# Forget-gate sums a slot later, drains ahead of a split, a second head-norm bank and sums placed later in a two-block fp32 transformer kernel

## The chip, the cores and the metric

One core of one Trainium2 chip runs the whole program. The metric is the device time of one launch in microseconds, taken as the median of several runs; smaller is better. The engines are TensorE (PE in the profile, with its weight loads as PEld), VectorE (DVE), ScalarE (ACT), GpSimd (POOL) and SyncE (SP, which here only issues DMAs). Each engine runs its own queue in order, and engines wait for each other by semaphores.

## The reference

Two transformer blocks over 256 tokens of width 1024, in float32, batch 1:

```python
def first_block(...):
    mod = silu(c) @ w_ada + b_ada                      # shift, scale, gate, twice
    u = rms_norm(x, ln1) * (1 + scale1) + shift1
    x = x + gate1 * mixer_sublayer(u, ...)             # gated conv + SSD scan, 32 heads
    u2 = rms_norm(x, ln2) * (1 + scale2) + shift2
    x = x + gate2 * (square(relu(u2 @ w_up)) @ w_down)
    return rms_norm(x, final_norm)

def second_block(...):
    fq, fk, fv, fg, dq, dk, dv = split(modulate(x) @ w_in)
    # q and k are normalised per head of 64; log_f = log_sigmoid(fg + b_f), its cumulative
    # sum over the tokens biases the 8 forget-gate ("fox") heads; 4 differential heads
    x = x + g1 * (concat(fox_out, diff_out) @ w_out)
    y = (silu(h2 @ w_gate) * (h2 @ w_up)) @ w_down
    return x + g2 * y
```

In the mixer, `dt = softplus(... + dt_bias)` steps the scan and `dt * a` is summed cumulatively over the tokens. The scan's output `y` times `silu(z)` is normalised in 8 groups of 256 channels before it meets `w_ssm_out`.

## The kernel before

Everything is kept transposed: channels on the 128 partitions, tokens along the row. `plan()` lays the weight products out as one list of steps. A step is one weight tile of 1024 rows by 256 columns (1 MB), made of two halves (`nb` 0 and 1) of 128 output columns. Each float32 product is three matmuls on numbers split into a high and a low part, so a half is 8 blocks x 3 = 24 matmuls, and a step 48.

Every engine's program walks the same list, `for n in range(NS)` and `for nb in range(NB)`; what it does there is its order in its queue, written out by hand. For a step n, SP brings the tile into one of three `raw` buffers, ACT makes `w_hi` (`split_hi`), DVE makes `w_lo` (`split_lo`), in general two steps ahead. PE takes a bank of PSUM (`take` waits until the previous content has been read out), multiplies, and signals `acc_ready` for each half; ACT and DVE then read ("drain") the bank. Three banks `acc0` to `acc2` go round, with the small banks M0 to M4 for everything else.

The steps in order, with the names that are used below: `xbc` 0 to 15 (scan inputs; `X0`), `cc`/`cx`/`cb` 0 to 3, two pairs `gc`/`co`, `z` 0 to 7 (`Z0`), two more pairs `gc`/`co`, then four times `gs`, `so`, `so`, then `wo` 0 to 3, `up` 0 to 15 (`U0`), `dn` 0 to 3 with four steps each (`D_LAST` is the last), `dq` 0 (`I0`), `dk` 0, `fg` (`FG`, 8 columns only), `dq` 1, `dk` 1, `fq` 0, `fk` 0, `fq` 1, `fk` 1, `dv` 0 and 1, `fv` 0 and 1, `o2` 0 to 3, `gt`/`u2` alternating (`G0`), `d2`.

The places that the change touches:

- **dt**: after half 1 of `xbc` 3 PE computes the 32 dt rows; ACT copies them; PE transposes them (L1355); DVE adds the bias (`dt_z`, L1617); after step `SOFT_AT` (`xbc` 5) ACT and DVE share the softplus (L801 to L804 and L1440 to L1449).
- **z_sum**: eight sums over partitions (L1305) of squares that POOL has added in pairs (L665), one for each step from `z` 2 on.
- **Late norms**: the first two steps of `up` and of `gt`/`u2` multiply a not yet normalised input (`gxh`, `gxl`); `x_sum` (L1080, L1082) adds the squares between their products, ACT makes the inverse root `mx` (L753, L754), and DVE applies it.
- **Tail of dn**: `x_sum_ahead` (L1056 to L1059) adds the first seven blocks' squares, which POOL has summed in `rt` (L613), and `x_sum(2)` (L1073 to L1076) the last one's, followed by `keep_busy(7)`, fill matmuls.
- **Head norms**: after half 0 of the step behind each q or k step PE sums squares per head into M0 (L1339); ACT takes the root (L753, L754), DVE reads M0 again (L1693) and scales q or k (to L1702).
- **Forget gate**: softplus after step `FG + 2` (`dk` 1) ends in `dta`; PE's cumulative sums into M4 (L1371 to L1374); ACT copies them out (L1011); DVE writes `fcum` and `fcum_t` (L1708 to L1712).
- **attn_slot**: `at` counts the halves from `dq` 0 on. Scores (L1257 to L1262) come in slots 6, 8, 12, 14, 16, 18, 20 and 22, and DVE and ACT handle the softmax in the same slots.

Of the kernel before, what the change touches and what calls it, by code (L numbers as in the profile page):

```python
# [34 lines left out]
HD = 64  # L35
# [158 lines left out]
def build(nc, a, out):  # L194
# [36 lines left out]
    for k, kind in enumerate(("up", "gt")):  # L231
        for m in range(2):
            LATE[start_of[kind] + m] = 2 * k + m
    LATE_NORM = (1, 4)
    GAIN_AT = {1: 1, 2: 2, 4: 3}
    NARROW, N_SETTLE = 32, 6
# [23 lines left out]
    with ExitStack() as ctx, ExitStack() as programs:  # L260
# [216 lines left out]
        def pv_bank(c):  # L477

            return PV_BANK[c if c < 4 else 4 + (c - 4) // 2]

        def split_late(n):

            return I0 <= n < start_of["o2"]
# [225 lines left out]
        def _(act):  # L709
# [162 lines left out]
            for n in range(NS):  # L872
# [3 lines left out]
                if n == 1:  # L876
                    act.wait_ge(S("dt_in"), 16)
                    act.activation(dt_hi[:, :, :], dt_raw[:, :, :], ACT.Copy).then_inc(S("dt_hi"), 1)
                if (s.kind, s.j) in (("wo", 2), ("dn", 3), ("o2", 2)) and s.last:
                    log_exp_table()  # L880
# [11 lines left out]
                for nb in range(NB):  # L892
# [60 lines left out]
                    if nb == 0 and prev in ("dq", "dk", "fq", "fk"):  # L953
                        jq += 1
                        act.wait_ge(S("qsum_done"), jq)
                        if jq > 1:
                            act.wait_ge(S("qk_done"), NB * (jq - 1))
                        inverse_root(qr, M0[:, :], HD, "qroot")

# [46 lines left out]
                    if n == FG + 1 and nb == 0:  # L1006
                        act.wait_ge(S("acc_ready"), steps[FG].g + NB)
                        act.activation(cv[0:8, 0, :], BANK[steps[FG].banks[0]][0:8, 0:T], ACT.Copy).then_inc(S("fg_t"), 1)
                    if n == FG + 3 and nb == 1:
                        act.wait_ge(S("fc_done"), 1)  # L1010
                        act.activation(fcum_t[0:2 * HEADS, P:3 * P], M4[0:2 * HEADS, T:2 * T], ACT.Copy)\  # L1011
                           .then_inc(S("fcum_hi"), 1)
# [29 lines left out]
        def _(pe):  # L1042
# [113 lines left out]
            def products(n, nb):  # L1156

                size = steps[n].group
                if steps[n].kind == "fg":
                    for i in range(4 * nb, 4 * nb + 4):  # L1160
                        product_part(n, 0, i)
                elif n in PAIRED:
                    if nb == 0:
                        for i0, i1 in ((0, PAIRED[n]), (PAIRED[n], KB)):
                            for b in range(NB):
                                for i in range(i0, i1):
                                    product_part(n, b, i)
                elif size == 1:
                    for i in range(steps[n].kts):
                        if n == D_LAST and nb == NB - 1 and i == KB - 2:  # L1170
                            x_sum_ahead()
                        product_part(n, nb, i)
                        if n in SETTLE_AT and nb == 0 and i == 0:
                            settle(n)
                if size > 1 and nb == 0:
                    if size == 3:
                        for i in range(6):
                            first_part(0, 0, i)
                            first_part(0, 1, i)
                            if i < 5:  # L1180
                                keep_busy(3)
                        for i in range(6):
                            first_part(1, 0, i)
                            first_part(1, 1, i)
                        for i in range(6, KB):
                            for m, b in ((0, 0), (0, 1), (1, 0), (1, 1)):
                                first_part(m, b, i)
                    order = [(m, b, i) for i in range(KB) for m in range(n + NAT * (size == 3), n + size) for b in range(NB)]
                    if n in LATE:
                        order = [(m, b, i) for m in (n, n + 1) for i in range(KB) for b in range(NB)]  # L1190
                    for m, b, i in order:
                        if n in LATE and (m, b, i) == (n, 0, 3):
                            x_sum(LATE_NORM[LATE[n] // 2])
                        product_part(m, b, i)
# [115 lines left out]
            for n in range(NS):  # L1310
                s = steps[n]
                for nb in range(NB):
                    products(n, nb)
                    if nb == 0 and 2 <= n - Z0 < 10:
                        z_sum(n - Z0 - 2)
# [19 lines left out]
                    if nb == 0 and n and steps[n - 1].kind in ("dq", "dk", "fq", "fk"):  # L1335
                        take("M0")
                        pe.wait_ge(S("qsq"), NB * (jq + 1))
                        jq += 1
                        pe.matmul(M0[:, :], blk64[:, :], sq[:, 2:4, :].rearrange("p a b -> p (a b)"), start=True, stop=True)\  # L1339
                          .then_inc(S("qsum_done"), 1)  # L1340
                        free["M0"] = ("qsum_read", jq)
                    if split_late(n):
                        attn_slot(NB * (n - I0) + nb)
                    if n == 3 and nb == 1:
# [6 lines left out]
                        ins.then_inc(S("dt_mm"), 1)  # L1351
                    if n == 4 and nb == 1:
                        pe.wait_ge(S("dt_t"), 1)
                        for t in range(TT):
                            ins = pe.transpose(M0[:, T + t * HEADS:T + (t + 1) * HEADS], gt[0:HEADS, 0, t * P:(t + 1) * P],  # L1355
                                               ident[0:HEADS, 0:HEADS])
                        ins.then_inc(S("dt_tr"), 1)
                        free["M0"] = ("dt_z", 1)
                    if n == FG + 2 and nb == 0:
# [4 lines left out]
                        ins.then_inc(S("fg_tr"), 1)  # L1364
                    if n == FG + 3 and nb == 1:
                        pe.wait_ge(S("nlf_done"), 1)
# [9 lines left out]
                        free["M4"] = ("fcum_done", 2)  # L1376
                if s.kind == "dn" and s.j == 3 and s.last:
                    x_sum(2)
                    keep_busy(7)
# [6 lines left out]
        def _(dve):  # L1386
# [165 lines left out]
            for n in range(NS):  # L1552
                s = steps[n]
                if n + 2 < NS and not split_late(n) and s.kind != "xbc" and not adds_tokens(n) and n not in LATE and n != D_LAST:
                    split_lo(n + 2)
# [15 lines left out]
                for nb in range(NB):  # L1571
# [25 lines left out]
                    if s.kind == "xbc":  # L1597
# [15 lines left out]
                        if nb == 0 and n != 2:  # L1613
                            split_lo(n + 3 if n < 2 else n + 2)
                        if nb == 0 and n == 5:
                            dve.wait_ge(S("dt_tr"), 1)
# [51 lines left out]
                    if s.kind == "up":  # L1668
# [4 lines left out]
                        else:  # L1673
                            late_f(i, nb)
                    if s.kind == "u2":
                        i = HID2 + NB * s.j + nb
# [13 lines left out]
                    if nb == 1 and prev and prev.kind in ("dq", "dk", "fq", "fk"):  # L1690
                        jq += 1
                        dve.wait_ge(S("qroot"), jq)
                        ins = dve.scalar_tensor_tensor(qt, M0[:, :], HD * EPS, qr, ALU.add, ALU.mult)  # L1693
                        ins.then_inc(S("qsum_read"), 1)
# [9 lines left out]
                    if split_late(n):  # L1704
                        attn_slot(NB * (n - I0) + nb)
                    if n == FG + 3 and nb == 1:
                        dve.wait_ge(S("fcum_hi"), 1)
# [92 lines left out]
```

## Time and profile before

| | |
|---|---|
| time, median of 3 runs | 928.96 us (927.3 to 930.58) |
| the profiled execution | 927.08 us, its span 925.3 us |
| PE busy | 890.7 us, 96% of the span |
| DVE busy | 678.6 us, 73% |
| ACT busy | 543.0 us, 59% |
| POOL busy | 289.4 us, 31% |
| mean granted clock of TensorE | 0.996 |
| mean DMA rate | 219 GB/s |

Times in the trace are microseconds from the start of the span. "Idle before" is the time in which an engine did nothing ahead of an instruction, with the engine, tile and line that ended it. Durations of matmuls are modelled and overlap; their starts tell how fast PE goes.

### The profile page before, as it was taken

The numbers are of one execution on the slowest core, as the hardware profiler recorded it, in microseconds if no ns is written. First come the engines' busy times: TensorE is split into PE (matmuls) and PEld (weight loads), VectorE is DVE, ScalarE is ACT, GpSimd is POOL, SyncE is SP. The second block draws the span as 40 slices with busy tenths as digits, with TensorE's granted clock in tenths as the row PEclk, the third lists the DMA queues.
The fourth block names the chain that finished last, engine by engine and source line by source line (L and its number), as shares of the span: only waits on it lengthen the run. The fifth ranks groups of instructions, "written<-read, shape, count | busy, mean of one in ns | idle before, by whom it ended". The sixth has DMA issues, their size and how long they took to land.

```text
span 925.3 us, 17831 instructions
## 1 busy us (share of the span) xinstructions
PE 890.7 (96%) x7390; PEld 858.2 (93%) x7390; DVE 678.6 (73%) x870; ACT 543.0 (59%) x840; POOL 289.4 (31%) x266
## 2 busy tenths in 40 slices
PE   5999999999999999998999999889999999999998
PEld 5899999999999999998999999878888999999998
DVE  5989997887776777768788767578995586755442
ACT  4477656457877864476656443467687674544431
POOL 5600003444377711176654111120003552212100
PEclk9999999999999999999999999999999999999999
DMA  9754555666686778854888887423233448755560
GB/s 366 292 212 175 183 205 206 229 234 248 233 301 222 262 262 291 290 184 141 306 300 286 300 319 282 162 92 134 95 137 108 166 147 325 269 208 180 174 225 24
DMA packets 36112, 203.02 MB, mean 219 GB/s; under 512 B 4928, under 2 KB 6080, under 8 KB 17216
## 3 DMA queue, kind: packets, MB, share of 16 engines
q1 hardware_dynamic: 36032, 201.89, 61.1%
q8 instruction: 58, 0.95, 0.4%
q14 instruction: 22, 0.18, 0.1%
HBM read 200.82 MB, written 1.05 MB: 218 GB/s over the span
## 4 chain that ended last, share of the span: by engine, by line
PE 63%; issue 14%; DVE 11%; POOL 5%; ACT 5%; DMA 1%; SPq 0%; ACTq 0%; POOLq 0%; DVEq 0%
PE acc L1140 55%; ACT w_hi L716 2%; DVE w_lo L1400 2%; DVE ada_w L1458 2%; DVE cv L1603 2%; POOL rt L613 1%; DMA ada_w<-in_ada_tiles 1%; PE m L1140 1%; PE m L1225 1%; POOL ysl L619 1%; DVE qk L1702 1%; POOL maps L660 1%; POOL ul L619 1%; PE acc L1105 1%; DVE maps L1696 1%
## 5 line engine op out<-in xcount | busy, mean ns | idle before, releaser
L1400 DVE TENSOR_TENSOR w_lo<-raw,w_hi 128x2048 fp32r<-128x2048 f32 x141 | 323.7, 2296 | 134.7 <-ACT w_hi L716 134.7
L1140 PE MATMUL acc<-uh,w_hi 128*128 128x256 f32 x1320 | 373.6, 283 | 4.2 <-DVE fr L1672 2.3
L1140 PE MATMUL acc<-ul,w_hi 128*128 128x256 f32 x1320 | 367.0, 278 | 0.0
L1140 PE MATMUL acc<-uh,w_lo 128*128 128x256 f32 x1320 | 366.9, 278 | 0.0
L716 ACT ACTIVATE w_hi<-raw 128x2048 fp32r<-128x2048 f32 x141 | 266.2, 1888 | 78.9 <-PE acc L1140 78.9
L1140 PEld LDWEIGHTS acc<-uh,w_hi 128*128 128x128 f32 x1320 | 249.5, 189 | 10.4 <-issue 5.4
L1140 PEld LDWEIGHTS acc<-ul,w_hi 128*128 128x128 f32 x1320 | 249.4, 189 | 0.4 <-issue 0.2
L1140 PEld LDWEIGHTS acc<-uh,w_lo 128*128 128x128 f32 x1320 | 249.3, 189 | 0.0
L1140 PE MATMUL acc<-hidh,w_hi 128*128 128x256 f32 x432 | 119.4, 276 | 0.0
L1140 PE MATMUL acc<-hidl,w_hi 128*128 128x256 f32 x432 | 119.2, 276 | 0.0
L1140 PE MATMUL acc<-hidh,w_lo 128*128 128x256 f32 x432 | 119.2, 276 | 0.0
L1765 DVE CUSTOM_DVE_ANT_0 colw<-colw,cact,par_all 128x1024 f32<-128x1024 f32 x80 | 117.8, 1480 | 0.6 <-DMA colw<-in_ada_cols 0.6
L619 POOL TENSOR_TENSOR hidl<-fr,hidh 128x256 fp32r<-128x256 f32 x54 | 72.4, 1341 | 119.0 <-ACT hidh L725 119.0
L1140 PEld LDWEIGHTS acc<-hidh,w_hi 128*128 128x128 f32 x432 | 81.1, 188 | 0.0
L1140 PEld LDWEIGHTS acc<-hidl,w_hi 128*128 128x128 f32 x432 | 81.1, 188 | 0.0
L1140 PEld LDWEIGHTS acc<-hidh,w_lo 128*128 128x128 f32 x432 | 81.1, 188 | 0.0
L660 POOL TENSOR_TENSOR maps<-maps 128x384 f32<-128x384 f32 x16 | 21.1, 1317 | 113.0 <-ACT maps L993 112.9
L619 POOL TENSOR_TENSOR ycl<-fr,ych 128x256 fp32r<-128x256 f32 x16 | 19.3, 1208 | 82.0 <-ACT ych L725 82.0
L1603 DVE SCALAR_TENSOR_TENSOR cv<-acc,par_all,cv 128x255 f32<-128x255 f32 (+2 forms) x87 | 41.2, 480 | 4.8 <-ACT cv L913 2.4
L725 ACT ACTIVATE hidh<-fr 128x256 fp32r<-128x256 f32 x54 | 22.2, 411 | 34.4 <-DVE fr L1680 27.0
L613 POOL TENSOR_TENSOR rt<-rt,sq 128x256 f32<-128x256 f32 x20 | 23.2, 1173 | 55.5 <-ACT sq L744 55.5
L1664 DVE SCALAR_TENSOR_TENSOR xT<-acc,mod,xT 128x256 f32<-128x256 f32 x31 | 14.4, 480 | 32.0 <-PE acc L1140 32.0
(368 smaller groups left out, 1603.7 us busy)
## 6 DMA issues: line engine op xcount, KB each, us to landing
raw<-in_tiles SPq DMA_DIRECT2D x137, 1024.0 KB, 5.6
colw<-in_ada_cols SPq DMA_DIRECT2D x80, 512.0 KB, 5.3
ada_w<-in_ada_tiles SPq DMA_DIRECT2D x8, 1024.0 KB, 17.0
raw<-in_rest SPq DMA_DIRECT2D x4, 768.0 KB, 4.6
cact<-in_c_rows SPq DMA_DIRECT2D x2, 512.0 KB, 4.2
xT<-in_x SPq DMA_DIRECT2D x1, 1024.0 KB, 7.3
first_w<-in_tiles SPq DMA_DIRECT2D x1, 1024.0 KB, 17.1
out<-xT SPq DMA_DIRECT2D x8, 128.0 KB, 3.8
```

Source lines behind the costliest of these rows:

```text
L613: pool.tensor_tensor(rt[:, x, :], first, sq[:, k % 4, :], ALU.add).then_inc(S("sq_added"), 1)
L619: pool.tensor_tensor(lo, uf[:, i, :] if i < YC else fr[:, i % NF, :], hi.bitcast(F32), ALU.subtract).then_inc(S("act_lo"), 1)
L660: pool.tensor_tensor(EXS[q % 4], EXS[q % 4], sc[:, q // 4 % 2, :], ALU.mult).then_inc(S("mul_done"), 1)
L716: act.activation(w_hi[:, n % NHL, 0:s.kts, 0:s.cols], raw_of(n), ACT.Copy)\
L725: act.activation(hi, x, ACT.Copy).then_inc(S("act_hi"), 1)
L1105: ins = pe.matmul(out_, raw_of(n)[:, i, nb * P:(nb + 1) * P], uf[:, i, :], start=(i == 0), stop=(i == KB - 1))
L1140: ins = pe.matmul(o, l, r, start=(s.k == 0 and i == 0 and not j), stop=(s.last and i == s.kts - 1 and j == 2))
L1400: dve.tensor_tensor(lo, raw_of(n), hi.bitcast(F32), ALU.subtract).then_inc(S("lo_ready"), 1)
L1458: dve.tensor_tensor_reduce(w, w, cact[:, :], 1.0, ada_b[:, c:c + 1], ALU.mult, ALU.add, mod[:, c:c + 1]).then_inc(S("ada_sum"), 1)
L1603: ins = dve.scalar_tensor_tensor(cv[:, i % 2, o:T], ps[:, 0:T - o], ssm_w[:, 32 * tap + fb:32 * tap + fb + 1], cv[:, i % 2, o:T], ALU.mult ...
L1664: dve.scalar_tensor_tensor(xT[:, b, :], ps, GATE[gate][:, b:b + 1], xT[:, b, :], ALU.mult, ALU.add).then_inc(S("x_ready"), 1)
L1765: dve.tensor_tensor_reduce(w, w, cact[:, :], 1.0, ada_b[:, c:c + 1], ALU.mult, ALU.add, mod[:, c:c + 1]).then_inc(S("col_sum"), 1)
```

## The change

It moves work in the queues and adds no arithmetic. `n == 4`, half 1, becomes `n == 5`, half 0, for PE's transposes of dt, and DVE's bias goes from half 0 to half 1 of step 5. Every `z_sum` goes from half 0 to half 1 of its step. `x_sum` in the first `gt` step stands before block 7 and not before block 3 (in `up` it stays). The split for `up` 4 goes from the start of DVE's step `up` 2 to its end. `x_sum_ahead` goes from inside the last dn half to behind it, and ACT loads the table for the roots one step earlier. The second head norm (`dk` 0) uses M4. The forget gate's cumulative sums go from half 1 of `fq` 0 to half 0 of `fk` 0 on PE, ACT and DVE.

```diff
     LATE_NORM = (1, 4)
+    SUM_AT = (3, 7)
...
+        def Q_BANK(jq):
+
+            return ("M4", M4) if jq == 2 else ("M0", M0)
...
-                if (s.kind, s.j) in (("wo", 2), ("dn", 3), ("o2", 2)) and s.last:
+                if n == D_LAST - 1 or (s.kind, s.j) in (("wo", 2), ("o2", 2)) and s.last:
                     log_exp_table()
...
-                        inverse_root(qr, M0[:, :], HD, "qroot")
+                        inverse_root(qr, Q_BANK(jq)[1][:, :], HD, "qroot")
...
-                    if n == FG + 3 and nb == 1:
+                    if n == FG + 4 and nb == 0:
                         act.wait_ge(S("fc_done"), 1)
...
-                        if n == D_LAST and nb == NB - 1 and i == KB - 2:
-                            x_sum_ahead()
                         product_part(n, nb, i)
...
-                        if n in LATE and (m, b, i) == (n, 0, 3):
+                        if n in LATE and (m, b, i) == (n, 0, SUM_AT[LATE[n] // 2]):
                             x_sum(LATE_NORM[LATE[n] // 2])
...
-                    if nb == 0 and 2 <= n - Z0 < 10:
+                    if nb == 1 and 2 <= n - Z0 < 10:
                         z_sum(n - Z0 - 2)
...
-                        take("M0")
-                        pe.wait_ge(S("qsq"), NB * (jq + 1))
                         jq += 1
-                        pe.matmul(M0[:, :], blk64[:, :], sq[:, 2:4, :].rearrange("p a b -> p (a b)"), start=True, stop=True)\
+                        name, bank = Q_BANK(jq)
+                        take(name)
+                        pe.wait_ge(S("qsq"), NB * jq)
+                        pe.matmul(bank[:, :], blk64[:, :], sq[:, 2:4, :].rearrange("p a b -> p (a b)"), start=True, stop=True)\
                           .then_inc(S("qsum_done"), 1)
-                        free["M0"] = ("qsum_read", jq)
+                        free[name] = ("qsum_read", jq)
...
-                    if n == 4 and nb == 1:
+                    if n == 5 and nb == 0:
                         pe.wait_ge(S("dt_t"), 1)
...
-                    if n == FG + 3 and nb == 1:
+                    if n == FG + 4 and nb == 0:
                         pe.wait_ge(S("nlf_done"), 1)
...
                 if s.kind == "dn" and s.j == 3 and s.last:
+                    x_sum_ahead()
                     x_sum(2)
                     keep_busy(7)
...
-                if n + 2 < NS and not split_late(n) and s.kind != "xbc" and not adds_tokens(n) and n not in LATE and n != D_LAST:
+                if n + 2 < NS and not split_late(n) and s.kind != "xbc" and not adds_tokens(n) and n not in LATE and n not in (D_LAST, U0 + 2):
                     split_lo(n + 2)
...
-                        if nb == 0 and n == 5:
+                        if nb == 1 and n == 5:
                             dve.wait_ge(S("dt_tr"), 1)
...
+                        if n == U0 + 2 and nb == NB - 1:
+                            split_lo(n + 2)
...
-                    if n == FG + 3 and nb == 1:
+                    if n == FG + 4 and nb == 0:
                         dve.wait_ge(S("fcum_hi"), 1)
```

## Rows read from the trace of the kernel before

**Rows 1.** Waits of PE, longest in total first: us in total, times, longest.

```profile
PE m L1305 <- POOL sq L665: 2.8, 3, 1.3
PE m L1080 <- POOL rt L613: 2.5, 1, 2.5
PE m L1339 <- DVE maps L1693: 2.4, 1, 2.4
PE acc L1140 <- DVE fr L1672: 2.3, 1, 2.3
PE m L1372 <- DVE dta L1736: 1.8, 1, 1.8
...
PE m L1355 <- ACT gt L1005: 1.2, 1, 1.2
```

**Rows 2.** Timeline of DVE, xbc stage: start, duration, instruction.

```profile
72.42 0.22 DVE L1617 TENSOR_TENSOR cct<-m,par_all 128x64 f32<-128x64 f32 x1
72.55 1.51 DVE L1603 SCALAR_TENSOR_TENSOR cv<-acc,par_all,cv 128x255 f32<-128x255 f32 x3
```

**Rows 3.** Timeline of PE in the xbc stage; in brackets the idle before.

```profile
83.65 0.36 PE L1140 MATMUL acc<-uh,w_hi 128*128 128x256 f32 x1 [0.61 <-DVE cv L1603]
```

**Rows 4.** Timeline of DVE, split for the second gs step.

```profile
339.05 2.29 DVE L1400 TENSOR_TENSOR w_lo<-raw,w_hi 128x2048 fp32r<-128x2048 f32 x1 [1.89 <-ACT w_hi L716]
```

**Rows 5.** Timeline of PE, first matmul of the second gs step.

```profile
342.20 0.28 PE L1140 MATMUL acc<-uh,w_hi 128*128 128x256 f32 x1
```

**Rows 6.** Timeline of ACT and DVE, step up 2.

```profile
436.31 0.37 ACT L937 ACTIVATE gt<-acc 128x256 f32<-128x256 f32 x1
...
435.88 2.29 DVE L1400 TENSOR_TENSOR w_lo<-raw,w_hi 128x2048 fp32r<-128x2048 f32 x1 [1.63 <-ACT w_hi L716]
```

**Rows 7.** Timeline of PE, POOL and DVE, tail of dn.

```profile
595.28 0.67 PE L1056 MATMUL m<-rt,ones 128*128 128x256 f32 x2 [1.41 <-POOL rt L613]
...
596.22 0.59 PE L1059 MATMUL m<-rt,ones 128*128 128x256 f32 x2
...
598.55 0.70 PE L1073 MATMUL m<-sq,eps_ones 128*128 128x256 f32 x2 [1.02 <-ACT sq L744]
...
592.95 2.88 POOL L613 TENSOR_TENSOR rt<-rt,sq 128x256 f32<-128x256 f32 x2 [16.43 <-ACT sq L744]
...
592.28 2.28 DVE L1400 TENSOR_TENSOR w_lo<-raw,w_hi 128x2048 fp32r<-128x2048 f32 x1
```

**Rows 8.** Timeline of DVE and PE, head norm of dk 0.

```profile
625.71 0.88 DVE L1702 SCALAR_TENSOR_TENSOR qk<-qk,par_all,rt 128x256 f32<-128x256 f32 x2
...
626.64 0.38 PE L1260 MATMUL m<-qk 64*128 64x128 f32 x2
```

**Rows 9.** Timeline of DVE, ACT and PE, slots 12 to 20.

```profile
654.55 0.55 DVE L1531 SCALAR_TENSOR_TENSOR maps<-dist_ts,m 128x384 f32<-128x384 f32 x1 [1.11 <-PE m L1262]
...
656.78 0.68 DVE L1693 SCALAR_TENSOR_TENSOR maps<-m,rt 128x512 f32<-128x512 f32 x1
...
657.70 0.19 ACT L851 ACTIVATION_READ_ACCUMULATOR maps<-maps,nmx 128x1 f32 x1
...
685.15 0.44 PE L1257 MATMUL m<-fcum_t,pick 128*128 128x384 f32 x1 [0.30 <-DVE qk L1702]
```

**Rows 10.** Stretches: busy PE, PEld, DVE, ACT, POOL; granted clock; DMA share, GB/s.

```profile
656.78:685.10 28.32, 28.07 (x220) 24.65 (x219) 27.61 (x60) 23.32 (x62) 0.00 (x0) 1.00 0.35 125
...
648.40:651.70 3.30, 3.30 (x17) 3.30 (x17) 3.17 (x8) 0.95 (x2) 0.00 (x0) 0.50 0.00 0
```

**Rows 11.** Timeline of POOL, DVE and PE, first gt and u2 steps.

```profile
741.63 1.32 POOL L639 TENSOR_TENSOR gxl<-cct,gxh 128x256 fp32r<-128x256 f32 x2
...
752.32 4.14 POOL L619 TENSOR_TENSOR ul<-fr,uh 128x256 fp32r<-128x256 f32 x3 [1.36 <-ACT uh L725]
...
745.03 0.87 DVE L1424 SCALAR_TENSOR_TENSOR fr<-xT,gain,mx 128x256 f32<-128x256 f32 x2
...
756.52 0.38 PE L1140 MATMUL acc<-uh,w_hi 128*128 128x256 f32 x1
```

More of the change, by code:

```diff
@@ L1692, in _ @@
                         dve.wait_ge(S("qroot"), jq)
-                        ins = dve.scalar_tensor_tensor(qt, M0[:, :], HD * EPS, qr, ALU.add, ALU.mult)
+                        ins = dve.scalar_tensor_tensor(qt, Q_BANK(jq)[1][:, :], HD * EPS, qr, ALU.add, ALU.mult)
                         ins.then_inc(S("qsum_read"), 1)
```

## The prediction

> **What bounds the kernel now.** I read the page first. PE is busy for 96% of the span and every other engine for less, so the end moves only when PE stands still for a shorter or longer time. Then I read PE's waits [rows 1]. The change aims at seven of them: 2.8 us for the sums in the z stage, 2.5 for the sum of squares in gt, 2.4 for the bank of the second head norm, 2.3 for a bank in up, 1.8 for the forget gate, 1.2 for dt, and 1.4 in the tail of dn [rows 7]. That is 14.4 us. A wait of PE that goes is time won only if nothing else makes PE wait before it has caught up. So I went through DVE, ACT and POOL in order of time around each place, and asked which of them had just been in time for PE. In five of the seven places one of them had.
>
> **dt, one slot later: a loss of 1.4.** PE no longer waits for ACT's copy (1.2). But DVE was the engine behind: its instructions follow each other there without a gap, and PE later waits for a bank that DVE drains, at 83.65 [rows 3]. DVE's bias addition, L1617, ran at 72.42, ahead of the convolution of half 1 (three instructions, 1.51 from 72.55 [rows 2]). It now comes behind them, so it ends 1.44 later, at about 74.1. ACT's softplus, with its two table loads, starts only then, DVE waits for ACT's exponential, and the whole exchange moves by 1.44, the next drain with it. PE's bank comes free at 83.65 + 1.43 = 85.1, whatever PE won before. Cost +1.43. The bound on the good side is the wait itself, -1.2; on the bad side +1.5.
>
> **z_sum, half a step later: a gain of 1.25.** All three waits (2.8) go, as POOL's pair is ready half a step later in each case. What is late next is the exchange between ACT and DVE from `z` 6 to the second `gs`. ACT splits a tile, DVE splits it, DVE normalises a block, ACT takes its high part and goes on to the next tile without waiting for PE. It ends in the split for the second `gs`, from 339.05 to 341.34 [rows 4], and PE starts that step at 342.20 [rows 5]: only 0.86 of slack. The exchange starts when ACT has drained `z` 5, whose half 1 now comes 0.4 earlier, as no sum stands before it (an estimate: two sums take 0.94, from 595.28 to 596.22 [rows 7], and the last one's pass overlaps). So PE can gain 0.86 + 0.4 = 1.25. Bounds: 0.4 (only that part), 2.8 (all).
>
> **x_sum before block 7 in gt: nothing.** PE waited to 741.8. Now it goes on with blocks 3 to 5 (six matmuls each, 0.68), waits for block 6 of `gxl`, which POOL makes half way through its pair from 741.63 to 742.95 [rows 11], and then does the sums at about 743.1 to 744.1. It leaves the first gt step 1.5 earlier. The root then ends at about 745.1, where DVE was free at 745.03, which costs 0.1. But in the third step of the stage PE waits for the last block of `ul`, which POOL ends at 756.46; PE's matmul behind it is at 756.52 [rows 11]. That chain starts from DVE at 745.03, so the 1.5 is given back there. Cost +0.1, bounds -1.5 and +0.2.
>
> **Drains ahead of the split in up: a gain of 1.9.** DVE split from 435.88 to 438.17 although ACT had the second relu ready at 436.68 [rows 6]. With the drains first, PE's bank is free at about 436.5 and not 438.5. The split then runs from 437.1 to 439.4, and PE, at the end of its half at 439.3, waits about 0.15 for it. The next halves find their banks at 442.1 and 446.7, 0.1 and 0.9 before PE needs them. Gain 1.9. On the good side 2.05. On the bad side, POOL's low part of the same block may stand in the way of the split. One such short POOL operation is 0.66, half of the pair of 1.32 [rows 11], so my lower bound is 1.9 - 0.7 = 1.2. The Trainium skill (SBUF — State Buffer, Who interferes with whom) says that a DVE instruction with two SBUF inputs and a GpSimd instruction that reads SBUF contend for one shared read interface, and that whichever issues first keeps the other out. The trace agrees in kind: two POOL additions took 2.88 beside the split at 592.28 [rows 7]. By that rule it is the order of issue at 437.1 that chooses between 1.9 and 1.2.
>
> **Tail of dn: a gain of 1.9.** PE waited 1.4 for POOL, then ran three sums, and only then the last six matmuls of the last half. Now those matmuls follow at once: PE had stopped at 595.28 - 1.41 = 593.87, and six more take 0.7, so the half is complete at 594.6. DVE is free by then (its split ends at 594.56), drains, and ACT has both squares some 1.4 later (about 0.5 for each of the three), at 596.0. The three sums cannot start before 595.28, as POOL's first addition decides that, and are through 1.4 later: 595.28 to the third's start at 596.22, and half of those 0.94 once more. So `x_sum` starts at 596.7 and not at 598.55 [rows 7]. Gain 1.9. What follows (root, DVE, ACT, POOL, first product of dq) hangs on it and moves with it. The table load an earlier step has free time on ACT and takes 0.1 off a square that POOL could not add sooner anyway: nothing. Bounds 1.4 and 2.9.
>
> **Second head-norm bank: nothing.** PE no longer waits for DVE's read of M0, but then for ACT's second square, so that more than half of the 2.4 stays. And the next scores need the q and k that DVE ends at 626.59; PE started them at 626.64 [rows 8]. DVE and ACT reach that time without PE's help (each root waits for DVE to be through with the last one). So PE waits there for what it had won. Bounds -0.9 and 0.
>
> **Forget-gate sums: a cost of 0.4.** PE goes straight into the next half, and does not lose the stretch from 648.4 to 651.7 at a granted clock of 0.50, the lower level of 1.2 GHz, that followed its wait [rows 10]; that was worth 1.65 more. Then it waits for DVE's k, about 1.2. DVE no longer waits for PE's scores (1.11 before 654.55 [rows 9]) and has no `fcum` work ahead of them (0.8, an estimate: three small instructions like L1617's 0.22 [rows 2], one of them wider), so it does them from 652.65 on, and is through 2.23 later (654.55 to 656.78), at 654.9. But in the same slot it now waits for ACT's copy of the sums. ACT ended its exponentials 1.1 after that point (657.89 against 656.78 [rows 9]), and the copy takes another 0.37, like the relu of [rows 6]. That puts DVE at 656.35, and with the 0.8 at 657.15 instead of 656.78. From there to 685.1 DVE is busy 27.61 of 28.32 us [rows 10], and PE waits for it at 685.15 [rows 9]. So PE is ahead for a while, and 0.4 late at 685.15. Bounds: -3.4 (wait and slow clock, all kept) and +2.3 (DVE's scores stay where they were, and 1.1 + 0.37 + 0.8 come on top).
>
> **The sum.** +1.43 - 1.25 + 0.1 - 1.9 - 1.9 + 0 + 0.4 = -3.1 us. The profiled execution took 927.08, 1.88 less than the median of the runs, 928.96. So 927.08 becomes 924.0, and the median 925.9 (-0.33%). 0.3% is 2.8 us; about that can be told from no change.
>
> **Rivals.**
> 1. *The waits stay away.* If DVE, ACT and POOL start sooner because PE does, most of the 14.4 is won, with the 1.65 of slow clock on top: 16 in the extreme, 6 to 10 if half holds: 919 to 923. For it: DVE has free time elsewhere (73%). Against: no free time just behind these places [rows 10].
> 2. *Given back.* The forget gate's wait on DVE costs its upper bound, 2.3 and not 0.4. The rest is -3.5, so -1.2: 927.8. For it: DVE has no slack up to 685. Against: DVE's wait for PE's scores should go.
> 3. *Slower, by the clock.* The change moves PE's idle time rather than removing it: about 1.5 before the dta sums near 77, 1.6 near 83.5, 1.2 near 649, 1.5 near 755. The granted clock fell to 0.50 behind the forget gate's wait for 3.3 us, which costs PE 1.65 [rows 10]. After the longer waits in up and gt no such stretch shows. One such fall where PE has no slack costs 1.65; two just cancel the gain, and the result is slower by over 0.3% with four: 925.9 + 6.6 = 932.5. Against: most of the new idle times lie where PE waits for DVE anyway, so a fall is covered.
>
> **How the numbers follow.** Forecast, 925.9, with its own range 923.5 to 928 from the smaller bounds: 0.55. Rival 1: 0.17. Rival 2: 0.22. Rival 3: 0.06. The range from 919.5 to 929.0 leaves out the better part of rival 1 and rival 3, and takes in the 1.6 by which runs of one kernel differ from their median. Faster by over 0.3%, that is below 926.2: 0.35 of the forecast and all of rival 1, 0.52. Within 0.3%: 0.20 of the forecast, rival 2 and a little of rival 3, 0.43. Slower: 0.05.
>
> **What would show it.** Right: no wait at L1355 and L1305, half of it at L1056, and none at L1339 for DVE; in their place a longer wait for DVE's cv at the fourth stretch of xbc (about 85), waits at the dta sums (about 77.4 to 79), before the second `gs` for `w_lo`, at L1260 for DVE's qk, and for `ul` in the third gt step. DVE's first softplus instruction near 76 and not 74.5. L1073 about 1.4 behind L1056 and not 3.3. DVE waiting for ACT's copy at L1708 for 1.3 to 1.5. Wrong: if PE does not wait longer at 83.65, or if DVE has more idle time between the forget-gate copy and the last k than before, then the exchange was not the bound and rival 1 is nearer.

## The result, and the profile after

The changed kernel takes 924.28 us (median of 6 runs, 923.1 to 925.48); the kernel before took 929.09 in the same comparison. The ratio is 0.9939, 95% interval 0.992 to 0.9958, so between 3.9 and 7.4 us faster. The prediction was 925.9, with a range from 919.5 to 929.0.

The two profiled executions differ by less: 927.08 against 925.48 us (spans 925.3 and 923.5). Why, the experiments show.

PE's waits after the change, longest in total first (us in total, times, longest), which answer to [rows 1]. The first belongs to the start of the kernel, and both kernels have it:

```profile
PE m L1073 <- ACT sq L749: 9.5, 1, 9.5
PE m L1263 <- DVE qk L1709: 3.7, 2, 2.5
PE m L1343 <- ACT sq L952: 2.1, 3, 1.7
PE acc L1145 <- POOL ul L624: 1.9, 4, 1.1
...
PE m L1260 <- DVE qk L1709: 1.5, 2, 1.0
PE acc L1145 <- DVE cv L1608: 1.4, 2, 0.7
...
PE m L1326 <- DVE dta L1735: 0.7, 1, 0.7
...
PE m L1343 <- DVE maps L1700: 0.5, 1, 0.5
```

The waits for POOL at the z sums and for ACT's dt copy are gone, the one for `fr` is 0.3 and the one at `x_sum_ahead` is 0.7. New ones stand in their place: for DVE's q and k (scores), for `dta`, for `ul`, and 0.7 for `gxl` in gt. No wait for `w_lo` stands before the second `gs` step, where I had announced one.

DVE in the dt exchange (start, duration, instruction; in brackets the idle before). The bias now stands behind the convolution, and the softplus starts at 75.87:

```profile
72.34 1.51 DVE L1608 SCALAR_TENSOR_TENSOR cv<-acc,par_all,cv 128x255 f32<-128x255 f32 x3
73.77 0.22 DVE L1622 TENSOR_TENSOR cct<-m,par_all 128x64 f32<-128x64 f32 x1
75.87 0.20 DVE L1445 TENSOR_SCALAR cct<-cct 128x64 f32<-128x64 f32 x1 [1.89 <-ACT cct L807]
```

The z stage: DVE's split that answers to [rows 4] (the second line), the split before it, and PE's first matmul of the second `gs` step, which answers to [rows 5]. PE starts that step before the split of [rows 4] is through:

```profile
335.45 2.29 DVE L1405 TENSOR_TENSOR w_lo<-raw,w_hi 128x2048 fp32r<-128x2048 f32 x1 [2.29 <-ACT w_hi L721]
...
339.63 2.29 DVE L1405 TENSOR_TENSOR w_lo<-raw,w_hi 128x2048 fp32r<-128x2048 f32 x1 [1.89 <-ACT w_hi L721]
...
341.13 0.28 PE L1145 MATMUL acc<-uh,w_hi 128*128 128x256 f32 x1
```

Step `up` 2, which answers to [rows 6], DVE and PE. The drains come first, two splits follow back to back, POOL's low part stands beside them, and PE waits 0.32:

```profile
435.71 1.00 DVE L1677 TENSOR_TENSOR fr<-acc,gt 128x256 f32<-128x256 f32 x2 [1.89 <-ACT gt L942]
436.63 2.32 DVE L1405 TENSOR_TENSOR w_lo<-raw,w_hi 128x2048 fp32r<-128x2048 f32 x1
...
438.87 2.82 DVE L1405 TENSOR_TENSOR w_lo<-raw,w_hi 128x2048 fp32r<-128x2048 f32 x1
...
436.76 2.78 POOL L624 TENSOR_TENSOR hidl<-fr,hidh 128x256 fp32r<-128x256 f32 x1
...
436.19 0.38 PE L1145 MATMUL acc<-uh,w_hi 128*128 128x256 f32 x1 [0.32 <-DVE fr L1677]
```

The tail of dn, which answers to [rows 7]. The last block's sums follow 1.37 behind the first, and not 3.27:

```profile
593.38 0.67 PE L1061 MATMUL m<-rt,ones 128*128 128x256 f32 x2 [0.73 <-POOL rt L618]
...
594.75 0.59 PE L1078 MATMUL m<-sq,eps_ones 128*128 128x256 f32 x2
```

Head norm of `dk` 0, first scores, forget gate and third pair of fox scores (PE, then DVE), which answer to [rows 8, 9]:

```profile
615.44 1.10 PE L1343 MATMUL m<-sq,blk 128*128 128x512 f32 x2 [1.66 <-ACT sq L952]
623.13 0.49 PE L1263 MATMUL m<-qk 64*128 64x128 f32 x4 [2.50 <-DVE qk L1709]
...
646.26 1.13 PE L1343 MATMUL m<-sq,blk 128*128 128x512 f32 x2 [0.46 <-DVE maps L1700]
648.62 0.49 PE L1263 MATMUL m<-qk 64*128 64x128 f32 x4 [1.24 <-DVE qk L1709]
...
683.58 0.61 PE L1260 MATMUL m<-fcum_t,pick 128*128 128x384 f32 x2 [1.02 <-DVE qk L1709]
...
654.31 0.17 DVE L1715 TENSOR_SCALAR fcum<-m 128x16 f32<-128x16 f32 x1 [1.32 <-ACT fcum_t L1016]
```

Behind the wait of 2.50 the granted clock fell. The kernel before had its falls elsewhere: the one of [rows 10], and one behind the wait of 2.41 at the second head norm, which neither [rows 10] nor the prediction names. Columns as there, the changed kernel and then the kernel before:

```profile
623.10:631.20 8.10, 8.07 (x57) 7.74 (x58) 7.03 (x11) 4.65 (x14) 0.00 (x0) 0.79 0.38 131
```

```profile
621.10:624.50 3.40, 3.40 (x19) 2.74 (x17) 1.86 (x5) 2.32 (x3) 0.00 (x0) 0.50 0.62 260
```

### The profile page after: what moved, and what is told of

Its sections match the earlier page's. It is cut to its first block, busy times and chain, and to the rows that moved or that the text cites. A ratio compares the mean times of both kernels' runs of the same rounds, so it can differ in the third digit from the quotient of the medians.

```text
span 923.5 us, 17831 instructions
## 1 busy us (share of the span) xinstructions
PE 893.2 (97%) x7390; PEld 860.8 (93%) x7390; DVE 678.7 (73%) x870; ACT 542.7 (59%) x840; POOL 290.4 (31%) x266
## 4 chain that ended last, share of the span: by engine, by line
PE 62%; issue 13%; DVE 11%; ACT 5%; POOL 4%; DMA 3%; SPq 1%; POOLq 0%; ACTq 0%; DVEq 0%
PE acc L1145 57%; DMA raw<-in_tiles 3%; DVE w_lo L1405 3%; ACT w_hi L721 2%; DVE cv L1608 2%; POOL rt L618 1%; POOL ul L624 1%; PE m L1228 1%; DVE qk L1709 1%; DVE fr L1429 1%; POOL maps L665 1%; SPq L537 1%; DVE maps L1703 1%; DVE rt L1704 1%; DVE maps L1700 1%
## 5 line engine op out<-in xcount | busy, mean ns | idle before, releaser
L1145 PE MATMUL acc<-ych,w_hi 128*128 128x256 f32 x128 | 36.4, 284 | 0.9 <-POOL ycl L624 0.9
```

The costliest lines, as they stand in the source:

```text
L1145: ins = pe.matmul(o, l, r, start=(s.k == 0 and i == 0 and not j), stop=(s.last and i == s.kts - 1 and j == 2))
```

## The experiments

Twelve kernels were run, each timed against the kernel before. To read their traces I cut the span at seven starts of PE that every kernel has (lines of the changed kernel): the last product of the scan (L1231), the first of the settling matmuls in the step before the second `gs` (L1159), the sums of `up` (L1085), the first sum of dn's tail (L1061), the first head norm and the third (L1343), the third pair of fox scores (L1260). Each length is the difference of two starts in one profiled execution, in us. Bold marks a stretch whose queue differs from the changed kernel's; `best_fill`, told below, is left out:

| kernel | to scan's end | z | gs, so, wo | up, dn | tail, dq | head norm, scores | forget gate | rest |
|---|---|---|---|---|---|---|---|---|
| before | **262.1** | **74.29** | 79.82 | **179.04** | **19.55** | **18.24** | **52.08** | **240.2** |
| changed | 263.6 | 71.76 | 80.47 | 177.56 | 17.92 | 19.88 | 52.40 | 239.9 |
| z_back | 263.7 | **74.28** | 80.47 | 177.59 | 17.92 | 19.83 | 52.42 | 240.5 |
| up_back | 264.1 | 72.07 | 80.49 | **179.58** | 17.93 | 18.43 | 52.40 | 239.8 |
| dn_back | 264.4 | 71.76 | 79.81 | 177.56 | **19.92** | 19.85 | 52.42 | 239.9 |
| bank_back | 263.4 | 72.08 | 80.48 | 177.90 | 17.92 | **18.24** | 52.40 | 240.5 |
| dt_mixed | **262.0** | 71.75 | 79.82 | 177.56 | 17.92 | 19.72 | 52.42 | 239.9 |
| exch_twice | 263.4 | 71.75 | **82.95** | 177.90 | 17.55 | 18.43 | 52.40 | 239.9 |
| best | **262.1** | 71.74 | 80.47 | 177.57 | 17.55 | 18.23 | **50.99** | **240.8** |
| best_fg_late | **261.9** | 71.76 | 79.81 | 177.56 | 17.55 | 19.86 | 52.42 | **241.5** |
| best_gt_late | **262.1** | 72.08 | 79.83 | 177.56 | 17.54 | 19.87 | **53.64** | 240.0 |
| best_fill_short | **262.1** | 71.74 | 80.47 | 177.90 | 17.92 | **18.24** | **50.99** | **239.6** |
| before_fill | **262.0** | **74.27** | 80.47 | **180.68** | **19.93** | **18.22** | **50.99** | **239.8** |

The last column is that kernel's span less the rest. Unmarked entries of a column differ by what one execution differs from another; the two sizes in which most of that comes (0.3 to 0.65, and 1.6) are told below.

**One part undone at a time.** `z_back`: the eight sums in half 0 again.

```diff
-                    if nb == 1 and 2 <= n - Z0 < 10:
+                    if nb == 0 and 2 <= n - Z0 < 10:
```

> The changed kernel with the eight sums of the z stage back in half 0 of their steps, and nothing else undone. Theory of the trace: PE reaches the second gs step 2.7 us later (that is what the two traces show between the dt stage and that step), so the time is 2.7 us above that of the changed kernel, and the three waits at the sums, 2.8 in all, are back. Rival, the prediction's step: the exchange between ACT and DVE that ends in the split at 339 gives only 1.25, so +1.25 in time, and PE waits for w_lo in the changed kernel. Nothing changes ahead of z.

927.56 us (12 runs), ratio to the kernel before 0.997 (0.9956 to 0.9985). The three waits, 2.8 in all, are back, and the z stretch is 2.52 longer. The changed kernel's z gain is 2.5, twice my term.

`up_back`: DVE's split for `up` 4 at the start of its step again.

> The changed kernel with DVE's split for up 4 back at the start of its step up 2. Theory: the wait of PE for the bank that DVE drains is 2.3 again and not 0.3, the following halves start 1.9 later, and as no engine is just in time behind it (PE is without a wait for over 100 us) the whole 1.9 shows at the end. Rival: the 1.9 is given back by some 0.5 in the stretch from there to the tail of dn, where the changed kernel's matmuls started a little farther apart, so 1.4 in time.

926.61 us (11 runs), 0.9969 (0.9954 to 0.9984). Stretch +2.02, PE's wait 2.12 again, and nothing of it comes back later.

`dn_back`: `x_sum_ahead` inside the last half again, table load one step later.

```diff
+                        if n == D_LAST and nb == NB - 1 and i == KB - 2:
+                            x_sum_ahead()
...
-                    x_sum_ahead()
                     x_sum(2)
```

> The changed kernel with the tail of dn as before: the early sums inside the last half and the table load one step later. Theory: the last block's squares are summed 1.9 later (3.3 and not 1.4 behind the first sum of rt), all that follows up to the first product of dq moves with it, and PE's later waits for ACT and DVE move too, so +1.9 at the end. Rival: the exchange for the first scores (PE waits 2.5 there in the changed kernel) does not depend on that start and takes part of it back: +0.5 or less.

927.07 us (11 runs), 0.9971 (0.9958 to 0.9984). Stretch +2.00, kept to the end. The rival falls: the exchange before the first scores starts at what this tail ends.

`bank_back`: `Q_BANK` always gives M0.

> The changed kernel with the second head norm's sums in M0 again. Theory, the prediction's 0: PE waits for DVE's read of M0 (2.4 and not 1.7) and so comes 0.8 later to the next product, but has 2.5 us of waiting before the first scores, where the 0.8 is gone; the scores start at the same time. Rival: the shorter wait before the first scores changes how often the slow clock follows there, by up to 1.7 in single runs.

924.37 us (4 runs), 0.9942 (0.9921 to 0.9964), as the changed kernel. The stretch is 18.24 as in the kernel before and in `best`, which has the second bank and no slow clock there: where the clock does not fall, the bank is worth nothing. It does change what a fall costs. With M0 PE stands 2.41 at the head norm, and then has some 1.7 of waiting left before the first scores (`before_fill`, which has no fall here, waits 1.69). In this run and in the kernel before the clock fell behind the 2.41, and the slower matmuls used up that wait:

```profile
616.72 2.08 PE L1343 MATMUL m<-sq,blk 128*128 128x512 f32 x2 [2.41 <-DVE maps L1700]
623.63 0.38 PE L1263 MATMUL m<-qk 64*128 64x128 f32 x2
```

```profile
616.55:619.90 3.35, 3.18 (x9) 1.45 (x10) 2.38 (x5) 2.06 (x3) 0.00 (x0) 0.50 0.79 281
```

With M4 the long wait, 2.4 to 2.5, stands right before the first scores, and nothing behind it covers a fall: six of the nine traces with M4 and no fills have one there and are 19.7 to 19.9, three have none and are 18.2 to 18.4. That is the rival named above, and by the traces the second bank costs 1.6 in such executions. The medians, with four runs here, do not show it.

**dt: DVE's place or PE's?** `dt_mixed` leaves PE's transposes late and puts only DVE's bias back.

```diff
-                        if nb == 1 and n == 5:
+                        if nb == 0 and n == 5:
                             dve.wait_ge(S("dt_tr"), 1)
```

> The changed kernel with DVE's bias addition for dt back in half 0 of step 5, while PE's transposes stay in half 0 of step 5. Theory: it is DVE's place that costs, not PE's. The softplus starts 1.44 earlier, PE's wait for the bank near 83.65 ends 1.4 to 1.65 earlier, and the time is 1.4 to 1.65 below the changed kernel's. PE's waits at the dta sums (0.7) and at the dt transposes (none) stay small. Rival: the exchange is not what PE waits for (ACT's own work is), then 0 to 0.3. Second rival: DVE waits for PE's transposes, and the addition costs what it saves, 0.

923.81 us (6 runs), 0.9933 (0.9915 to 0.9952). The medians do not tell 1.4 us apart; the traces do: it reaches the end of the scan 1.4 to 1.6 before the kernels with the late bias that started like it. The bias and PE's wait for the bank in this run, and then that wait in `bank_back`, which has the late bias:

```profile
72.40 0.22 DVE L1622 TENSOR_TENSOR cct<-m,par_all 128x64 f32<-128x64 f32 x1
...
83.63 0.36 PE L1145 MATMUL acc<-uh,w_hi 128*128 128x256 f32 x1 [0.70 <-DVE cv L1608]
```

```profile
85.04 0.35 PE L1145 MATMUL acc<-uh,w_hi 128*128 128x256 f32 x1 [0.71 <-DVE cv L1608]
```

83.63 against 85.04 is 1.41, with PE's transposes in the same place. The bias's place alone costs it.

**The exchange in z, lengthened.** `exch_twice` does the split of 339.6 twice.

```diff
+                    if n == start_of["gs"] + 2:
+                        split_lo(n + 2, False)
                     split_lo(n + 2)
```

> The changed kernel, in which DVE does its 2.29 us split at 339.6 (right before PE's second gs step) twice over, the same values into the same tile. The prediction took this split as the one that PE waits for at the second gs step: then every later start of PE moves by 2.3 us, and a wait for w_lo of about that length stands before that step. Theory of the trace: the split belongs to the step after, PE needs it some 5 us later, and neither the second gs step nor the time moves (0 to 0.3).

926.08 us (10 runs), 0.9965 (0.995 to 0.9979). By the time alone the prediction's theory would stand: the stretch is 2.48 longer. The trace says otherwise. There is no wait for `w_lo`, and the z stretch, which ends just before, is the same 71.75. PE waits once, in the middle of the second `gs` step, for the bank that DVE drains behind the doubled split:

```profile
344.43 0.39 PE L1145 MATMUL acc<-uh,w_hi 128*128 128x256 f32 x1 [0.62 <-DVE cv L1666]
```

So a delay of 2.29 cost 0.62 of waiting: the drain has 1.67 of slack in the changed kernel, and the split itself more. The rest is PE's own pace behind that wait, at a granted clock of 1.00. As the median of the ten runs is 1.8 above the changed kernel's, it is not the chance of one execution; what ties the pace to the doubled split is not shown. The same 40 us, `exch_twice` and then the changed kernel:

```profile
350.00:390.00 40.00, 40.00 (x342) 40.00 (x341) 30.77 (x32) 17.35 (x16) 4.44 (x5) 1.00 0.86 303
```

```profile
350.00:390.00 40.00, 40.00 (x356) 40.00 (x355) 31.29 (x32) 16.13 (x16) 4.95 (x4) 1.00 0.89 307
```

342 matmuls instead of 356 in 40 us, 4% fewer; over the 53 us to the next wait that is about 2.1 us, of which 0.4 returns as a shorter wait there.

**Only the parts that won.** `best` puts DVE's bias, the forget gate's sums and `x_sum` in gt back, and keeps the rest.

```diff
-    SUM_AT = (3, 7)
+    SUM_AT = (3, 3)
...
-                        if nb == 1 and n == 5:
+                        if nb == 0 and n == 5:
...
-                    if n == FG + 4 and nb == 0:
+                    if n == FG + 3 and nb == 1:
```

(the last on PE, ACT and DVE)

> Only the parts that won are kept: z_sum later, the drains ahead of the split in up, the tail of dn, the second bank; DVE's bias for dt, the forget gate's sums and x_sum in gt go back to their old places. Sum of the parts by the traces: -1.6 (dt), -0.3 (forget gate, with its stretch of slow clock back), -0.25 (gt): 2.1 us below the changed kernel. Rival: without the two small costs behind 640 PE only waits for DVE again at the place where both kernels wait (685), so only the -1.6 of dt shows.

922.76 us (6 runs), 0.9918 (0.9901 to 0.9936); its fastest run of 921.38 is 1.7 below the changed kernel's fastest. It keeps M4 for the second head norm; a version without it was not run. Its forget-gate stretch is 1.41 shorter than the changed kernel's, more than I had expected. In gt the clock fell behind the wait of 2.32 before the sums:

```profile
735.31 0.67 PE L1085 MATMUL m<-rt,ones 128*128 128x256 f32 x2 [2.32 <-POOL rt L618]
...
735.90:740.00 4.10, 4.10 (x22) 4.05 (x21) 3.67 (x5) 2.23 (x6) 0.54 (x1) 0.58 0.68 252
```

**Forget gate, new place on that version.** `best_fg_late` has the sums at `FG + 4`, half 0, again.

> The kept-parts version, but with the forget gate's cumulative sums in their new place (half 0 of fk 0); so of the change only DVE's place for dt and x_sum in gt are undone. Between the head norm of dk 1 and the third pair of fox scores (the wait at 685) the kept-parts version needed 43.0 us, the changed kernel 44.5 and the kernel before 44.1 with 1.65 of slow clock in it. Theory (what the trace of before suggests): the old place costs nothing without its slow clock, the new place makes PE wait for DVE's k and for fcum, so this run is 1.4 slower there than the kept-parts version. Rival, the prediction's 0.4: the new place costs 0.3 to 0.4 and the rest is the clock. If the clock falls elsewhere, only the landmarks tell.

924.21 us (5 runs), 0.9942 (0.9922 to 0.9962). The stretch is 52.42 against 50.99, +1.43, and neither trace has slow clock in it. The column shows the whole pattern. In its new place the stretch is 52.40 to 52.42 in all eight traces, though in two of them (`up_back`, `dn_back`) the clock fell at 652: PE's waits for DVE behind it, up to the one before 683, cover it. In its old place it is 50.99 where the clock did not fall, 52.08 in the kernel before, where it fell once, and 53.64 in `best_gt_late`, where it stayed low from 642.8 to 650. So the move costs 1.4 and buys off a fall worth 1.1 to 2.7.

**x_sum in gt, new place on that version.** `best_gt_late`: `SUM_AT = (3, 7)`.

> The kept-parts version, but with x_sum in gt before block 7. Theory: nothing but the place of the wait changes; PE starts the matmul behind the last block of ul in the third step 0.1 to 0.25 later, as DVE's first normalisation starts by that much later. Rival: the wait before the sums, 2.3 us in one piece, is what the slow clock followed in the kept-parts version (736 to 740), and two waits of 0.7 and 1.1 do not bring it: then 1.5 faster where it had fallen.

922.86 us (5 runs), 0.9923 (0.9895 to 0.9951), as `best`. Without a fall the last column is 240.2 for the old place (the kernel before) and 239.8 to 240.5 for the new: nothing to tell apart. In `best` and `best_fg_late`, which wait 2.3 to 2.5 in one piece, a fall added 0.6 to 1.3. The slow stretch at the forget gate in this run, behind a wait of 1.78:

```profile
642.80:650.00 7.20, 7.20 (x34) 6.46 (x34) 6.38 (x10) 2.57 (x4) 0.31 (x1) 0.53 0.16 65
```

**Waits filled.** `best_fill` puts fill matmuls of `keep_busy` before three waits of `best`, 12, 20 and 18 of them.

> The kept-parts version with fill matmuls (ones by tri into the free bank M1, results unused) where PE waits longest: 12 ahead of the second head norm's sum (wait 1.6), 20 ahead of the first scores (2.45), 18 ahead of the sums in gt (2.3); they are meant to end before the wait does. Theory: the falls of the granted clock follow PE's waits, so with the waits filled none comes at these places; the mean granted clock rises by about 0.0018 for each fall that goes, and the median falls by up to 1.7 for each, so 1 to 2 us in all. Rival: the falls are not tied to the waits; then the clock stays, and the time is the same or slightly above.

935.18 us (5 runs), 1.0067 (1.0049 to 1.0085), slower: I had taken 0.11 us for one; it is 0.43 to 0.49 (three of them are the row with x6 below, 1.46 us, and five the row with x10, 2.32 us, as each counts twice). The fills ran past the waits. Its trace has no fall at the three filled places, and one, at 651, behind the wait of 1.78 that was not filled. It was repeated with the right number, and one wait more:

```diff
+                        if jq == 2:
+                            keep_busy(3)
                         pe.wait_ge(S("qsq"), NB * jq)
...
+                    if p == 0:
+                        keep_busy(5)
...
                         take("M4")
+                        keep_busy(4, M4)
                         pe.wait_ge(S("nlf_done"), 1)
...
+                    if n == 4:
+                        keep_busy(5)
                     pe.wait_ge(S("sq_added"), added_at(n, KB - 2) + 1)
```

> The kept-parts version with fewer fill matmuls, as one takes 0.43 us and not 0.11: 3 before the second head norm's sum, 5 before the first scores, 4 before the forget gate's sums (into M4), 5 before the sums in gt. Theory: they end inside the waits (1.6, 2.45, 1.8, 2.3), PE has no pause of over 1.1 us there, no slow clock follows, the mean granted clock rises from 0.997 to 0.999 or 1.0 and the median falls by 1 to 2 us. Rival: the slow clock comes anyway or elsewhere, and the time is the same.

920.88 us (6 runs, 919.93 to 921.39), 0.9906 (0.9889 to 0.9923), the fastest of all. The granted clock is 1.000 in each of the six runs. What is left of two of the waits:

```profile
612.47 1.46 PE L1097 MATMUL m<-tri,ones 128*128 128x256 f32 x6
614.17 1.13 PE L1349 MATMUL m<-sq,blk 128*128 128x512 f32 x2 [0.24 <-ACT sq L952]
619.23 2.32 PE L1097 MATMUL m<-tri,ones 128*128 128x256 f32 x10
621.95 0.49 PE L1267 MATMUL m<-qk 64*128 64x128 f32 x4 [0.40 <-DVE qk L1716]
```

```profile
core 0: 919.0 us, clock 1.000
```

`before_fill` does the same to the kernel before, at the second head norm (5), the forget gate (4) and gt (5).

> The kernel before, and nothing of the change, with fill matmuls in three waits: 5 before the second head norm's sum (wait 2.4), 4 before the forget gate's sums (1.8), 5 before the sums in gt (2.5). Theory: part of what the change won in the median (4.8 to 5.7 us, where the prediction's sum was 3.1) is slow clock behind such waits, which the kernel before has more of (mean granted clock 0.995 against 0.997); with the waits filled its clock rises to 0.997 or more and its time falls by 1.5 to 2.5 us, with PE's waits all still there. Rival: the difference in the clock comes from the places that aren't filled (the z sums, up, the tail of dn) and the time stays.

928.35 us (12 runs) against 929.44, ratio 0.9989 (0.9976 to 1.0001): by the medians a gain of some 1 us, less than expected, and the interval does not tell it from none. The mean clock is 0.998 over its runs, against 0.995 over the 60 runs of the kernel before that stood beside these experiments. Its forget-gate stretch is 50.99 and not 52.08. In up, where nothing was filled, the clock fell behind the wait of 2.26, and its stretch is 1.6 longer than that of the kernel before.

## Why the prediction was right, and where it was not

**dt.** Right to the tenth: predicted +1.43, measured 1.41 at the bank (85.04 against 83.63), with the softplus at 75.87. `dt_mixed` shows that it is DVE's place that costs, and that PE's could have moved for nothing. One sign failed: PE's wait at that bank is 0.71 in `bank_back` against 0.61 before, and not longer by what was lost. What PE won goes in three waits ahead of it, 0.7 for `cv` at 64, 0.6 for `dta` at 79 and 0.7 for `cv` at 81. In the profiled execution the clock had fallen at 82, so that PE reached the wait later and it doesn't show. Such a fall stands there in three of the six traces with the late bias, costs 0.2, and is in none with the early one.

**z_sum.** The direction was right; the size was wrong, -1.25 against -2.5. The failing step is "It ends in the split for the second `gs`, from 339.05 to 341.34 [rows 4], and PE starts that step at 342.20 [rows 5]: only 0.86 of slack." That split, which [rows 4] names wrongly too, serves the step behind: DVE works two steps ahead, and the changed kernel's PE starts the second `gs` at 341.13, inside the split. The split for the second `gs` is the one before, from 335.45, and ends 3.4 ahead of that start. What really comes next is the bank that DVE drains behind it, 1.67 away by `exch_twice`. So nothing was late next, and nearly the whole 2.8 of waiting was won. My upper bound held it. An engine had been just in time in four of the seven places, and not in five.

**up and the tail of dn.** Right: -1.9 each, measured 1.5 and 1.6 between the two profiled executions, and 2.0 each against `up_back` and `dn_back`. In up the first of DVE's two splits took 2.32, the 2.29 of [rows 6] but for 0.03, and the second 2.82. POOL's low part beside the first took 2.78, where one alone takes 0.75: it ended at 439.54, 0.6 behind the first split, and the second split had started at 438.87. So the contention named under SBUF — State Buffer, Who interferes with whom, in the Trainium skill, is there in kind, but it held up POOL and the second split, which PE does not wait for. The first, the one of the sum, lost nothing, and 1.9 was the value to take.

**Second head-norm bank.** 0 is right, for the reason given, where the clock does not fall: PE waits 2.50 for the same q and k. The bound of 0 on the bad side was wrong. The prediction did not see that the kernel before has a fall of the clock behind its 2.41 (621.1 to 624.5), paid out of the wait for q and k. With M4 the fall comes behind that wait, in six of nine traces, and costs 1.6.

**Forget gate.** The sum was +0.4 and the two traces give +0.32 (52.40 against 52.08). The steps held one by one: DVE waits 1.32 for ACT's copy, PE 1.24 for k. The number is a difference of two, and the experiments show both: 1.4 of cost, less a fall of the clock that was worth 1.1 here, as 0.5 of its 1.65 was covered by the wait at 685. So +0.4 held because the trace that was read had that fall in it; in an execution without one the move costs 1.4. What I missed is a wait for DVE's read of M0 at L1343 (0.46), which I had said would be gone.

**x_sum in gt.** Right: about 0, given back at `ul`, where PE now waits 1.1.

**The sum and the median.** With z at its true size the sum is -4.4, and the medians differ by 4.8. The pair of profiled executions shows only -1.6 (927.08 to 925.48), for two reasons that the table holds: the clock fell behind the wait for the first scores (+1.6), and the wo stage ran 0.65 longer. The second does not belong to the change: `dn_back` and `dt_mixed` have 79.8 in wo. The first does in part: whether the clock falls there differs from one execution to the next (`up_back` and `exch_twice` have the same queue there and 18.43), but that it costs time is the second bank's doing. Besides, the profiled execution of the kernel before is faster than each of its six runs, and the changed kernel's is the slowest of its six. The kernel before had one fall uncovered in that execution; over 60 runs its mean clock is 0.995, against 0.997 over the changed kernel's six, which is 2 us of span at a clock of 1 and some of it covered. So part of the gain in the median may be less slow clock; how much, and which of the changed places bring it, is not shown. z was 1.25 better than forecast, and in some executions the bank was 1.6 and the forget gate 1.0 worse; that such errors partly cancel in the median is luck.

**The rivals.** The waits that stayed away (rival 1) were three of seven, z, up and the tail of dn; where an engine was just in time (dt, head norm, forget gate, gt) they came back, as argued. Rival 2's price for the forget gate, 2.3, did not come. Rival 3 did come as a mechanism: two falls stand in the changed kernel's trace, one of them uncovered, behind a wait that it did not list. It did not decide the sign: one such fall costs 1.6 against three parts that win 2.0 to 2.5 each, and the kernel before has its own.

## What to carry to other kernels

When one engine prepares work two steps ahead, look up which step an instruction serves before calling it the one that is late next, and test it by lengthening it: the wait that appears names the true successor. Move PE's half of an exchange freely, but count the other engine's half by what stands ahead of it in its queue. A wait on PE can cost more than its length, and what a fall of the clock costs depends on whether another wait stands behind it: look there before moving a wait to the end of a chain. Where a wait can't be removed, a few harmless matmuls that end inside it made the clock and the time steady here, in six of six runs, once their duration was read from a row.

## What the runs showed of the hardware

The granted clock falls behind PE's waits in some executions and not in others, at the same place and after the same wait. Behind 2.44 to 2.51 us before the first scores it fell in six of the nine traces that have that wait, and not in `best`, `up_back` and `exch_twice`; the stretch is then 19.7 to 19.9 and not 18.2 to 18.4. Each fall costs about 1.65 us where nothing covers it, and nothing at the head norm in the kernel before and `bank_back`, where a wait of 1.7 stands behind it. It also followed waits of 2.41 (head norm in M0), 1.78 (forget gate, old place), 2.26 (up) and 2.32 and 2.52 (gt), and shorter ones: 1.24 (forget gate, new place, `up_back` and `dn_back`), and in the changed kernel, `up_back` and `dn_back` two waits of 0.6 to 0.7 within 3 us (dt). With four waits filled the mean clock was 1.000 in all six runs.

PE has a second, smaller loss behind short waits, at a granted clock of 1.00: product matmuls start every 0.118 us and not every 0.113, for 10 to 90 us on end. It began behind waits of 0.3 to 0.9, again in some executions only; other such stretches have no wait ahead of them (from 264 on in the changed kernel). Wo, by windows of the changed kernel and of the kernel before, 87 matmuls against 90 in 10 us, which is how 0.65 us went there:

```profile
400.00:410.00 10.00, 10.00 (x87) 10.00 (x86) 6.77 (x8) 8.86 (x16) 8.01 (x8) 1.00 0.31 113
```

```profile
400.00:410.00 10.00, 10.00 (x90) 10.00 (x89) 6.42 (x8) 9.19 (x15) 8.23 (x9) 1.00 0.32 107
```

What sets that pace was not found; `best_fill_short`, with the clock at 1.000, has it too.
